# First two modulation vectors in blocks of 512 columns, accumulated by TensorE, beside the first mixing

## The reference

```python
mod_all = jnp.einsum('bd,lde->lbe', jax.nn.silu(c), ada_w) + ada_b[:, None, :]   # ada_w: (2, 2048, 6 * 2048)
shift1, scale1, gate1, shift2, scale2, gate2 = jnp.split(mod_all[i], 6, axis=-1)
h = _rmsnorm(x) * (1 + scale1[:, None, :]) + shift1[:, None, :]
h_prev = jnp.pad(h, ((0, 0), (1, 0), (0, 0)))[:, :T]
xr, xw, xk, xv, xa, xg = (h + (h_prev - h) * mu[i] for i in range(6))
r = xr @ w_rkv[0]; k = xk @ w_rkv[1]; v = xv @ w_rkv[2]
```

## Time and profile before

| | |
|---|---|
| median of 3 runs | 2964.02 us (2958.07 to 2967.55) |
| the profiled execution, its own time | 2968.07 us |
| its span | 2966.5 us |
| TensorE busy, mean granted clock | 2695.2 us (91%), 0.946 |
| VectorE, ScalarE, GpSimd busy | 2008.4, 1320.7, 44.5 us |
| first matmul of r (L1167) | at 142.31 us |

### The profile page before, as it was taken

One profiled execution on the slowest core, in us unless ns is written; L12 is line 12 of the kernel. 1 busy time (PEld: TensorE's weight loads), 2 busy tenths in 40 slices (PEclk: granted clock), 3 DMA queues, 4 the chain that ended last, 5 costly groups with the idle time before them and its releaser, 6 DMA issues.

```text
span 2966.5 us, 55090 instructions
## 1 busy us (share of the span) xinstructions
PE 2695.2 (91%) x20605; PEld 2348.1 (79%) x20605; DVE 2008.4 (68%) x2597; ACT 1320.7 (45%) x2010; POOL 44.5 (2%) x88
## 2 busy tenths in 40 slices
PE   1299997699989899999999979989989999999998
PEld 1288875688878788888888868878778888888887
DVE  6778850688867777777777787654767755555556
ACT  1155542344444555444444444435445544444444
POOL 1000002000000000000000000000000000000000
PEclk6599998899999999999999999999989999999999
DMA  7669845434428678878788786832657866665653
GB/s 301 254 227 310 303 142 173 165 125 143 145 84 281 213 263 282 294 243 281 255 286 271 243 281 226 269 115 78 228 168 270 283 202 186 192 188 189 189 170 116
DMA packets 472655, 639.96 MB, mean 216 GB/s; under 512 B 21909, under 2 KB 427834, under 8 KB 451770
## 3 DMA queue, kind: packets, MB, share of 16 engines
q1 hardware_dynamic: 468666, 625.31, 63.2%
q0 software_dynamic: 3840, 12.59, 1.1%
HBM read 623.14 MB, written 14.68 MB: 215 GB/s over the span
## 4 chain that ended last, share of the span: by engine, by line
PE 62%; DVE 5%; ACT 2%; issue 1%; DVEq 0%; ACTq 0%
PE ps L1167 39%; PE ps L1168 20%; DVE wlo L1155 1%; PE ps L1214 1%; PE ps L862 1%; PE ps L853 1%; DVE nt L132 1%; ACT whi L1150 1%; DVE act L145 1%; DVE ada_acc L1200 1%; PE ps L889 0%; PE ps L1411 0%; DVE gsum L99 0%; DVE nt L930 0%; DVE x L317 0%
## 5 line engine op out<-in xcount | busy, mean ns | idle before, releaser
L1167 PE MATMUL ps<-act,whi 128*128 128x512 f32 x3808 | 1355.0, 401 | 40.6 <-DVE act L202 17.8
L1155 DVE TENSOR_TENSOR wlo<-raw,whi 128x1024 fp32r<-128x1024 f32 (+1 forms) x768 | 901.8, 1192 | 504.0 <-ACT whi L1150 501.4
L1168 PE MATMUL ps<-act,wlo 128*128 128x256 f32 x3808 | 1071.9, 281 | 0.0
L1150 ACT ACTIVATE whi<-raw 128x1024 fp32r<-128x1024 f32 (+1 forms) x768 | 774.8, 1030 | 666.0 <-PE ps L1168 663.9
L1167 PEld LDWEIGHTS ps<-act,whi 128*128 128x128 f32 x3808 | 724.4, 190 | 220.6 <-DVE wlo L1155 25.0
L1167 PE MATMUL ps<-hid,whi 128*128 128x512 f32 x2176 | 776.6, 399 | 11.9 <-DVE wlo L1155 9.0
L1168 PEld LDWEIGHTS ps<-act,wlo 128*128 128x128 f32 x3808 | 727.4, 191 | 0.0
L1168 PE MATMUL ps<-hid,wlo 128*128 128x256 f32 x2176 | 616.3, 283 | 0.0
L1167 PEld LDWEIGHTS ps<-hid,whi 128*128 128x128 f32 x2176 | 413.4, 190 | 113.3 <-DVE wlo L1155 11.2
L1168 PEld LDWEIGHTS ps<-hid,wlo 128*128 128x128 f32 x2176 | 412.7, 190 | 0.0
L1200 DVE SCALAR_TENSOR_TENSOR ada_acc<-ada_ring,sc,ada_acc 128x2048 f32<-128x2048 f32 x128 | 300.3, 2346 | 0.3
(11 more groups left out here) (273 smaller groups left out, 2313.5 us busy)
## 6 DMA issues: line engine op xcount, KB each, us to landing
raw<-in_f_w SPq DMA_DIRECT2D x480, 512.0 KB, 4.5
ada_ring<-in_ada_w SPq DMA_DIRECT2D x172, 1024.0 KB, 7.3
raw<-in_a_w_rkv SPq DMA_DIRECT2D x96, 512.0 KB, 5.2
raw<-in_b_w_in SPq DMA_DIRECT2D x56, 512.0 KB, 3.9
raw<-in_f_w SPq DMA_DIRECT2D x64, 384.0 KB, 4.0
first_ring<-in_ada_w SPq DMA_DIRECT2D x20, 1024.0 KB, 6.4
raw<-in_a_w_o SPq DMA_DIRECT2D x32, 512.0 KB, 4.7
raw<-in_b_w_o SPq DMA_DIRECT2D x32, 512.0 KB, 5.6
```

The costliest lines, as they stand in the source:

```text
L1150: self.nc.scalar.activation(self.whi[:, u % SPL, 0:n], self.raw[:, u, 0:n], ACT.Copy).then_inc(self.s("hi_ready"), 1)
L1155: self.nc.vector.tensor_tensor(self.wlo[:, u % SPL, 0:n], self.raw[:, u, 0:n], self.whi[:, u % SPL, 0:n].bitcast(F32), SUB).then_inc(self. ...
L1167: self.nc.tensor.matmul(o, hi[:, kk, c0:c1], src[:, k].rearrange("p a t -> p (a t)"), start=k == 0, stop=False)
L1168: last = self.nc.tensor.matmul(o[:, T:2 * T], lo[:, kk, c0:c1], src[:, k, 0, :], start=False, stop=k == ktotal - 1)
```

## The change

A phase `Prologue` takes the place of the two blocks and stands as the first phase in one block with r, k and v.

- **The loads.** The 32 MB come in 32 parts of 1 MB in another order: for each *quarter* of 512 columns, for each of the two vectors, four parts of four rows k each. A part is 512 columns of four rows, pieces of 2 KB. The ring of six stays. Part n is issued when TensorE has finished part n-6.
- **The accumulation.** VectorE has none of it any more. For each part TensorE does sixteen matmuls with the part itself as weights (128 x 128, float32) and one column of `sc` as the moving operand, accumulating into one column of PSUM each. In all 512 such matmuls, where there were 32. A matmul with eight columns of zeros clears the bank at the start of a quarter, and at its end TensorE waits for its own last part.
- **The squares.** One tile at a time, 16 matmuls of 256 columns on TensorE with two buffers between ScalarE and TensorE, eight of them after part 2 and eight after part 4. `sqfirst` goes.
- **Quarters.** When both vectors' 512 columns are there, VectorE adds the bias, four tiles are modulated and mixed (`quarter_act`, `quarter_dve`).
- **The seam.** TensorE does 30 parts, then units 0 to 2 of r's first pair, then the last two parts, then waits for the last quarter before unit 3. On ScalarE and VectorE the last quarter stands behind the splitting of units 0 to 3 and ahead of that of units 4 to 7. The mixing is no longer the first phase's `prepare`.
- Semaphores of the start are counted in three (`first_vector`, `first_scalar`, `first_tensor`) and freed after v. ScalarE loads one activation table ahead. `x_odd` on VectorE stands behind the tables.

```diff
+    slots = 6
+    bank = (7, 5, 4, 6)
+    units = [(q, piece, kk) for q in range(4) for piece in range(2) for kk in range(4)]
+    last = 2
...
+    def sync(self, sp):
...
+        for n, (q, piece, kk) in enumerate(self.units):
+            if n == len(self.units) - self.last:
+                for u in range(4):
+                    p.load_unit(sp, u, self.first_phase["source"](0, u))
+            if n >= self.slots:
+                self.after_part(sp, n - self.slots)
+            at = piece * D + q * 512
+            sp.dma_start(p.first_ring[n % self.slots].rearrange("p (k n) -> p k n", k=4),
+                         view[:, 4 * kk:4 * kk + 4, at:at + 512]).then_inc(s(f"first_loaded{n % self.slots}"), 16)
+        for u in range(4, RAW):
+            p.load_unit(sp, u, self.first_phase["source"](0, u))
...
+    def quarter_act(self, act, q):
+        p, nc, s, m = self.p, self.p.nc, self.p.s, self.mixed
+        self.after_vector(act, "normed", KT)
+        act.wait_ge(s("mod_ready"), q + 1)
+        for k in (4 * q, 4 * q + 2):
+            nc.scalar.activation(p.hpad[:, k, 1:T + 1], p.hpad[:, k, 1:T + 1], ACT.Identity, scale=p.mod[:, 16 + k:17 + k],
+                                 bias=p.mod[:, k:k + 1]).then_inc(s("first_scalar"), 1)
+        for k in range(4 * q, 4 * q + 4):
...
+            m.m1(act, k, k)
+            if k > 4 * q:
+                m.copy(act, k - 1, (k - 1) % 4)
+        m.copy(act, 4 * q + 3, 3)
...
+    def quarter_dve(self, dve, q):
+        p, nc, s, m = self.p, self.p.nc, self.p.s, self.mixed
+        dve.wait_ge(s("ada_summed"), q + 1)
+        for piece in range(2):
+            at = 16 * piece + 4 * q
+            last = nc.vector.tensor_tensor(p.mod[:, at:at + 4], p.ps[:, self.bank[q], 4 * piece:4 * piece + 4],
+                                           p.pv[:, PV_ADA + at:PV_ADA + at + 4], ADD)
+        last.then_inc(s("mod_ready"), 1)
...
+        for k in range(4 * q, 4 * q + 4):
+            m.first(dve, k)
+            if k > 4 * q:
+                m.low(dve, k - 1)
+        m.low(dve, 4 * q + 3)
+
+    def part(self, pe, n):
+
+        p, nc, s = self.p, self.p.nc, self.p.s
+        q, piece, kk = self.units[n]
+        slot = n % self.slots
+        if n % 8 == 0:
...
+            nc.tensor.matmul(p.ps[:, self.bank[q], 0:8], p.ones[:], p.zeros[:], start=True, stop=False, skip_group_check=True)
+        pe.wait_ge(s(f"first_loaded{slot}"), 16 * (n // self.slots + 1))
+        for r in range(4):
+            for m in range(4):
+                last = nc.tensor.matmul(p.ps[:, self.bank[q], 4 * piece + m:4 * piece + m + 1],
+                                        p.first_ring[slot][:, r * 512 + m * P:r * 512 + (m + 1) * P], p.sc[:, 4 * kk + r:4 * kk + r + 1],
+                                        start=False, stop=n % 8 == 7 and r == 3, skip_group_check=True)
+        last.then_inc(s("first_tensor"), 1)
+        if n % 8 == 7:
+            self.after_part(pe, n)
+            pe.sem_inc(s("ada_summed"), 1)
+
+    def squares(self, pe, ks):
+        p, nc, s = self.p, self.p.nc, self.p.s
+        for k in ks:
+            self.after_scalar(pe, "squared", k + 1)
+            nc.tensor.matmul(p.ps[:, 6, 0:T], p.ones[:], p.tmp[:, k % 2, :], start=k == 0,
+                             stop=k == KT - 1).then_inc(s("first_tensor"), 1)
...
+        for n in range(len(self.units) - self.last):
+            self.part(pe, n)
+            if n in (2, 4):
+                self.squares(pe, range(8) if n == 2 else range(8, KT))
...
+    def last_quarter_pe(self, pe):
+        for n in range(len(self.units) - self.last, len(self.units)):
+            self.part(pe, n)
```

In `Linear`, TensorE's body of the first pair gains, ahead of unit 3:

```diff
+                    if self.arriving and g == 0 and q == 3 and starts:
+                        self.arriving.last_quarter_pe(pe)
                     if ready and g == 0 and starts:
                         ready.pe_wait(pe, kt * (q + 1))
```

More of the change, by code:

```diff
@@ L54 @@
 HEADS_ARMED = ("logits", "probs", "pturned", "barred_logits", "pT", "vh", "o_lo", "uk_turned", "vhp")
-PROLOGUE_ONLY = ("c_loaded", "rows_loaded", "x_loaded", "set", "ident", "blk", "mask_step", "masks", "sig_c", "silu_c", "x_even",
-                 "x_odd", "rows_turned", "x_turned", "pv", "one_more")
+PROLOGUE_ONLY = ("c_loaded", "rows_loaded", "x_loaded", "made", "first_vector", "first_scalar", "first_tensor", "first_loaded0", "first_loaded1",
+                 "first_loaded2", "first_loaded3", "first_loaded4", "first_loaded5")
 ARMED = frozenset(LINEAR_ARMED + HEADS_ARMED)
@@ L298, in dve_start @@
             self.p.nc.vector.memset(self.p.sqacc[:], 0.0).then_inc(self.p.s("sums_zeroed"), 1)
-            dve.wait_ge(self.p.s("sums_zeroed"), self.q0 // 8)
+            dve.wait_ge(self.p.s("sums_zeroed"), self.q0 // 8 + 1)
         self.p.mod_wait(dve, self.gate)
@@ L307, in act @@
         act.wait_ge(p.s("x_added"), i * 2 + (self.g0 + g + 1))
-        act.wait_ge(p.s("square_added"), i * 2 + (self.q0 + g))
+        if not (isinstance(i, int) and i * 2 + self.q0 + g == 0):
+            act.wait_ge(p.s("square_added"), i * 2 + (self.q0 + g))
         p.nc.scalar.activation(p.tmp[:], p.x[:, bass.ds(i * 4 + 2 * g, 2), :], ACT.Square).then_inc(p.s("squared"), 1)
@@ L321, in dve @@
             dve.wait_ge(p.s("squared"), i * 2 + (self.q0 + g + 1))
-            dve.wait_ge(p.s("square_added"), i * 2 + (self.q0 + g))
+            if not (isinstance(i, int) and i * 2 + self.q0 + g == 0):
+                dve.wait_ge(p.s("square_added"), i * 2 + (self.q0 + g))
             p.nc.vector.tensor_tensor(p.sqacc[:], p.sqacc[:], p.tmp[:], ADD).then_inc(p.s("square_added"), 1)
@@ L394, in __init__ @@
     def __init__(self, prog, phase, n, following, act_src, prepare=None, evac=None, ada=(), kt=UK, first_loaded=RAW, beside=(),
-                 ready=None):
+                 ready=None, arriving=None):
         p = self.p = prog
+        self.arriving = arriving
         self.phase, self.n, self.following, self.act_src, self.prepare, self.evac = phase, n, following, act_src, prepare, evac
@@ L465, in scalar @@
                 prepare.high(act, k)
+        if self.arriving:
+            self.arriving.last_quarter_act(act)
         def half(i):
@@ L512, in vector @@
                 prepare.low(dve, k)
+        if self.arriving:
+            self.arriving.last_quarter_dve(dve)
         for lo, hi, a in self.stretches:
@@ L967, in __init__ @@
         self.split_ahead = False
-        self.squares_at = [8, 16, 24, 32, 40]
-        self.squares = 8
+        self.squares_at = [0, 8, 16, 24, 32]
+        self.squares = 0
         self.glus = 0
@@ L1031, in layout @@
         self.cst, _ = place("cst", [P, 4])
+        self.zeros, _ = place("zeros", [P, 8])
         self.rstd, _ = place("rstd", [P, T])
@@ L1057, in layout @@
         self.gsum = v("gsum", [P, 2, 2, T], o_u + 12288)
-        self.sqfirst = v("sqfirst", [P, 2, T], o_split)
         self.proj = v("proj", [P, 28, T], o_u)
@@ L1419, in rstd_from_sums @@
         nc.scalar.activation(self.rstd[:], self.rstd[:], ACT.Exp, scale=-0.5).then_inc(s("rstd"), 1)
-    def modulate_first(self):
-        nc = self.nc
-        scale = lambda k: self.mod[:, 16 + k:17 + k]
-        shift = lambda k: self.mod[:, k:k + 1]
-        with nc.Block(no_gpsimd_drain=True) as block:
-            @block.scalar
-            def _(act):
-                for k in range(0, KT, 2):
-                    nc.scalar.activation(self.hpad[:, k, 1:T + 1], self.hpad[:, k, 1:T + 1], ACT.Identity, scale=scale(k), bias=shift(k))
-            @block.vector
-            def _(dve):
-                for k in range(1, KT, 2):
-                    nc.vector.tensor_scalar(self.hpad[:, k, 1:T + 1], self.hpad[:, k, 1:T + 1], scale(k), shift(k), MUL, ADD)
     def together(self, *phases):
@@ L2247, in build @@
         w_o = dict(source=self.unit_sources(I["a_w_o"][0]))
-        self.prologue(rkv[0])
-        if self.stop == 0:
-            return
-        local = [n for n in self.sems if n in PROLOGUE_ONLY or n.startswith("first_loaded")]
-        self.nc.clear_and_free_semaphores([self.sems.pop(n) for n in local])
-        self.modulate_first()
         halves = (self.act, self.hid, self.act)
         mixed = Mixed(self, 0, halves[0])
-        phases, before = [], None
+        arriving = Prologue(self, mixed, rkv[0])
+        phases, before = [arriving], arriving
         for q in range(3):
             after = Mixed(self, (2, 3)[q], halves[q + 1]) if q < 2 else MixedWhole(self, [(1, self.lmix[0]), (5, self.lmix[2])])
-            phases.append(Linear(self, rkv[q], 4, rkv[q + 1] if q < 2 else dict(source=lora_inner), halves[q], None if q else mixed,
-                                 ToScratch(self, q, 4), ([(2, 4, 32)], [(0, 4, 36)], [(0, 2, 44)])[q], beside=(after,), ready=before))
+            phases.append(Linear(self, rkv[q], 4, rkv[q + 1] if q < 2 else dict(source=lora_inner), halves[q], None,
```

(7 more changed lines are left out.)

349 lines of the change are left out of this document (185 added, 164 removed).

## The result

The changed kernel takes **3069.92 us** (median of 4 runs, 3066.27 to 3073.99) against 2965.78 us for the kernel before on the same chips. The ratio is 1.0346, with a 95% interval of 1.0306 to 1.0387: 3.5% slower. The forecast was 3071 us.

The account below looks back on a forecast made before the run. The prediction took VectorE's accumulations to bound the start, the loads close behind. Unit 3 at 262.9 in place of 157.7 us, plus 1.5 for its cold start, gave 107 us on 2964: 3071 us, with 8 in 10 for 3050 to 3092.

Parts of the forecast that it names:

- When the parts begin: Start of the stream on TensorE, when the transposes of x end: taken as 20.9 us.
- Which clock: TensorE's clock during the parts: half, 6.99 us a part, where full clock would give 3.63.
- Parts 0 to 29: TensorE's stream ahead of r's first units: 30 x 6.99 = 209.7 us, less 2.1 us at full clock.
- Squares: Two bursts of matmuls among the parts: 16.6 us, less 11.6 saved by full clock, 5.0 us net.
- Small things: Four clearing matmuls and three waits of TensorE at a quarter's end: 0 to 4 us, taken as 2.
- Parts 30 and 31: Last two parts, behind units 0 to 2: 14.0 us less 3.5 of full clock, ending at 256.8 us.
- The last quarter: Bias, modulation and mixing ahead of unit 3, with nothing to cover them: 6.1 us.
- Unit 3: The mark, behind which both kernels do the same work: start at 262.9 us, against 157.66 in the kernel before.
- The cold unit 3: Unit 3 begins at half clock and takes 4.6 us where it had 3.1: 1.5 us more.
- full clock throughout: Rival: TensorE keeps full clock in the stream, unit 3 at 166.5 us, 2973 us in all; chance 5 in 100.
- Loads set the pace: Rival: parts cost less than 3.63 us, loads bound them at 3.2 at most, 2931 us; chance 4 in 100.
- The clock comes and goes: Rival: half of the parts get full clock, each saving 3.4 us, 3021 us in all; chance 5 in 100.

Follow-up runs that it names:

- e1: The changed kernel with the moving column of the parts' matmuls repeated to 64 columns: 2975.7 us, 1.0022 of the kernel before.
- e4: The changed kernel with two of each part's four rows on VectorE, two on TensorE with 64 repeated columns: 2962.5 us, 0.9982 of the kernel before.
- e6: The changed kernel with three of each part's rows on VectorE, one on TensorE with a single moving column: 2943.8 us, 0.9915 of the kernel before.
- e8: The changed kernel with one of each part's rows on VectorE, three on TensorE with 64 repeated columns: 2955.6 us, 0.9960 of the kernel before.
- e9: e8 with parts 30 and 31 ahead of units 0 to 2 on TensorE: 2951.4 us, 0.9948 of the kernel before.
- e7: e6 with parts 30 and 31 ahead of units 0 to 2 on TensorE: 2945.8 us, 0.9912 of the kernel before.
- e5: The changed kernel with the accumulation given back to VectorE, 512 columns at a time: 2973.4 us, 1.0012 of the kernel before.

## Why the prediction was right

The mechanism was the one named: the stream of single-column matmuls ran at half clock and set the pace. That the time fell within 1 us of the forecast is luck, as the steps show:

- *When the parts begin:* 20.9 forecast, 20.25 measured.
- *Which clock:* half, read from bursts of 3.6 to 7 us in the earlier trace rows. The windows show 0.50 from 76 to 200 us without an exception, and e1 shows that this is the cause. The Trainium skill's rule ("TensorE: Matmul & The Clock Gate", "What's actually happening"), read as "a busy engine gets 2.4 GHz", would have given 2973. The measurement decides against that reading: TensorE was busy 59.69 of 60 us at 1.2 GHz.
- *Parts 0 to 29:* 6.99 us each forecast, 6.83 measured, as the last matmul's tail is paid once and not for each part: 4.8 us less. The first two parts saved 4.5 us in place of 2.1: behind the transposes the clock stayed full until 25.2, where with TensorE idle it had fallen at 23.0.
- *Squares:* 5.0 net forecast, 8.8 measured. They took 6.54 + 6.86 = 13.4 us and saved 2.7 + 1.9 in the parts behind them. Three errors are in it. At half clock a square's matmul takes 0.86 us (ScalarE, which follows TensorE square by square, starts five in 4.31 us from 37.50), not 1.035, as the 2.07 of the earlier trace rows has a tail in it: 2.8 less. The clock rose 6.0 and 5.5 us after the bursts began, at 42.2 and 59.3, not after 3.6, so the bursts themselves saved 0.4 in place of 4.6. And the parts behind them saved 4.6 in place of 7.0. The windows have the clock full for about 3.5 us in each of 39 to 50 and 50 to 64 (0.66 and 0.62), where the forecast had 8.2.
- *Small things:* 2 forecast; each quarter's end costs 0.87 us (two parts from 65.51 end at 79.16, the next begins at 80.03), about 2.7 in all.
- *Unit 0* at 235.5 forecast, 231.93 measured. *Units 0 to 2:* 10.8 and 10.75, by two errors that cancel: unit 0 took 5.1 us in place of 4.6, the next two 2.8 each in place of 3.1. *Parts 30 and 31:* 10.5 and 9.67. *The last quarter:* 6.1 and 5.66. *Unit 3:* 262.9 and 258.01.
- *The cold unit 3:* 1.5 forecast, 2.4 measured (5.3 against 2.9).

The errors of single terms are up to 5 us and of both signs; the mark was 4.9 us early. Medians differ by 104.1 us, the forecast said 107, and the kernel before was 1.8 us slower beside the changed one (2965.78) than in the median that the forecast was put on (2964.02). The prediction's "VectorE had 96 us for it all" is in none of its rows, which have the accumulation from 33.06 to 122.14, 89 us; its sum doesn't use it.

Of the rivals, "full clock throughout" was priced well: 2973 against e1's 2975.7, and unit 3 at 166.5 against 163.01. "Loads set the pace" was priced too high: the bound of 3.2 us a part came from pieces of 1 KB, but pieces of 2 KB run at 386 GB/s (e4, 23 to 40 us), 2.7 us a part. No kernel here reached that pace to the end; what e6 would win with it was not tried. "The clock comes and goes" was seen only in short stretches at the start, until 62.8, and not again before the seam.

## What to carry to other kernels

A matmul with one moving column was priced here by its weight load, and by the clock that the engine had when it ran: before moving a matrix-vector product to TensorE, look in the trace for a burst of the same instruction, and at the granted clock in and behind it. One column repeated to 64 cost nothing beside the weight load and kept the full clock in e1, e8 and e9, and lost it in e4 behind a wait. A split that needs no full clock (one row of four on TensorE, three on VectorE) did best. A wait ahead of the marked unit was worth removing only where the engine that waits also set when the work before it was done, as far as the marks of e7 and e9 show.

## What the hardware showed beyond that

- Streams of the same 64-column matmuls ran at 1.00 for 93 us in e1 (48.31 to 141.68) and 76 us in e8 (44.12 to 120.52), and at 0.50 for over 60 us in e4 after one wait of 1.38 us, both without a gap above 0.31 us. So in these runs the granted clock depended on what went before, not on the stream alone.
- `scalar_tensor_tensor` over 512 float32 columns costs 3.10 us a MB in e5, over 2048 columns 2.43.
- Loads in 2 KB pieces reached 386 GB/s in e4 at a DMA share of 1.05; the 8 KB pieces of the kernel before reached 434 at 1.04. So the quarters cost the loads some speed. The 372 GB/s of the earlier trace rows are no figure for 8 KB pieces: over half of the packets in that window are under 2 KB, most of them of r's first weights.
